# A two-block model kernel: retention's output products moved behind the next head, second weight units by operand tiles, and another order in the mixer

## What is computed

```python
# first block, per layer: h = h + mixer(norm(h)); h = h + cross_attention(norm(h)); h = h + conv_glu_ffn(norm(h))
lru_x, lru_g, m_x, m_o, m_if = split_cols(xn @ cd_w_in, CD_SIZES)      # mixer of layer 1
xc = causal_dwconv(lru_x, ...); gates = sigmoid(xc @ gate_w + gate_b)  # RG-LRU: linear recurrence
u = sqrt(-expm1(2.0 * log_a)) * (i_gate * xc)
h = linear_recurrence(exp(log_a), u) * gelu(lru_g)
xc = silu(causal_dwconv(m_x, ...)); q, k = headwise(xc, ...)           # mLSTM: gated attention, 4 heads
# second block, layer 1: retention
q, k, v = rope(z_q), rope(z_k), z_v                                    # 4 heads, qk 256, v 512 wide
o = rmsnorm(retention(q, k, v), out_norm)
o = o.reshape(B, S, nv) * silu(g)
return o @ w_out
# second block, feed forward
return (silu(h @ w_gate) * (h @ w_up)) @ w_down
```

## Time and profile before

| | |
|---|---|
| median of 3 runs | 3468.95 us (3465.75 to 3472.72) |
| profiled execution, its own time | 3469.26 us |
| its span, first to last instruction | 3467.4 us |
| PE busy | 3201.3 us (92%) |
| DVE busy | 1575.9 us (45%) |
| ACT busy | 1196.1 us (34%) |
| chain that ended last | PE 81%, DVE 12%, ACT 5% |
| mean granted TensorE clock | 0.955 |

### The profile page before, as it was taken

The page is one execution under the profiler, slowest core; times in us unless marked ns, Lnnn a source line. Parts: engine busy times, 40 slices in busy tenths (PEclk is TensorE's granted clock), DMA queues, the critical chain, the costliest instruction groups (busy, mean ns, idle before and its releaser), DMA issues.

```text
span 3467.4 us, 40278 instructions
## 1 busy us (share of the span) xinstructions
PE 3201.3 (92%) x17298; PEld 2530.7 (73%) x17298; DVE 1575.9 (45%) x2043; ACT 1196.1 (34%) x1621; POOL 115.0 (3%) x136
## 2 busy tenths in 40 slices
PE   7889888899999889999998797899999999989999
PEld 6787666678887656778875663678888778768887
DVE  4444456455443476355443426553335423453333
ACT  4343332343322464343223244532224232242221
POOL 1010000000000000000001000000000000000000
PEclk9999999999999999999999897899999999999999
DMA  4343001223332212133322120033323212223331
GB/s 142 112 142 81 20 26 38 73 61 98 99 89 85 77 61 79 43 85 97 97 84 71 55 86 0 22 88 97 97 85 110 73 64 76 85 59 100 98 97 61
DMA packets 344818, 270.34 MB, mean 78 GB/s; under 512 B 17040, under 2 KB 330640, under 8 KB 344384
## 3 DMA queue, kind: packets, MB, share of 16 engines
q1 hardware_dynamic: 340624, 252.30, 24.4%
q0 software_dynamic: 4016, 15.46, 1.3%
HBM read 261.45 MB, written 6.29 MB: 77 GB/s over the span
## 4 chain that ended last, share of the span: by engine, by line
PE 81%; DVE 12%; ACT 5%; issue 1%; POOL 0%; DMA 0%; DVEq 0%; SPq 0%; ACTq 0%; POOLq 0%
PE ps L192 80%; DVE arena L223 3%; DVE arena L215 3%; ACT arena L206 2%; DVE xlo L215 1%; PE ps L195 1%; DVE wlo L215 1%; ACT whi L209 1%; DVE split L215 1%; ACT split L209 1%; DVE sml L232 1%; DVE arena L219 1%; DVE hT L215 1%; ACT L206 0%; ACT arena L209 0%
## 5 line engine op out<-in xcount | busy, mean ns | idle before, releaser
L192 PE MATMUL ps<-xhi,whi 128*128 128x512 f32 (+4 forms) x2192 | 884.8, 404 | 55.5 <-DVE wlo L215 30.5
L192 PE MATMUL ps<-xhi,wlo 128*128 128x512 f32 (+4 forms) x2192 | 862.6, 394 | 0.0
L192 PE MATMUL ps<-xlo,whi 128*128 128x512 f32 (+4 forms) x2192 | 861.3, 393 | 0.0
L192 PE MATMUL ps<-split,whi 128*128 128x512 f32 (+4 forms) x2640 | 832.7, 393 | 26.6 <-DVE split L215 22.2
L215 DVE TENSOR_TENSOR wlo<-wraw,whi 128x2048 fp32r<-128x2048 f32 (+4 forms) x258 | 546.2, 2120 | 499.6 <-ACT whi L209 499.6
L192 PEld LDWEIGHTS ps<-split,whi 128*128 128x128 f32 (+3 forms) x2640 | 492.6, 190 | 157.6 <-issue 31.0
L209 ACT ACTIVATE whi<-wraw 128x2048 fp32r<-128x2048 f32 (+4 forms) x258 | 455.1, 1767 | 403.5 <-PE ps L192 383.5
L192 PEld LDWEIGHTS ps<-xhi,whi 128*128 128x128 f32 (+4 forms) x2192 | 414.1, 189 | 167.6 <-DVE wlo L215 33.9
L192 PE MATMUL ps<-split,wlo 128*128 128x512 f32 (+4 forms) x1320 | 511.4, 387 | 0.0
L192 PEld LDWEIGHTS ps<-xhi,wlo 128*128 128x128 f32 (+4 forms) x2192 | 414.4, 189 | 94.8 <-issue 7.3
L192 PEld LDWEIGHTS ps<-xlo,whi 128*128 128x128 f32 (+4 forms) x2192 | 413.5, 189 | 92.5
(11 more groups left out here) (103 smaller groups left out, 1994.9 us busy)
## 6 DMA issues: line engine op xcount, KB each, us to landing
wraw<-in_ffn_w_up SPq DMA_DIRECT2D x128, 512.0 KB, 5.2
wraw<-in_ffn_w_down SPq DMA_DIRECT2D x32, 1024.0 KB, 5.2
wraw<-in_odd_w_in SPq DMA_DIRECT2D x24, 1024.0 KB, 5.2
wraw<-in_ffn_w_gate SPq DMA_DIRECT2D x44, 512.0 KB, 4.0
wraw<-in_xattn_wkv SPq DMA_DIRECT2D x16, 1024.0 KB, 5.5
wraw<-in_xattn_wq SPq DMA_DIRECT2D x8, 1024.0 KB, 5.3
wraw<-in_xattn_wo SPq DMA_DIRECT2D x8, 1024.0 KB, 5.2
wraw<-in_cd_w_in SPq DMA_DIRECT2D x8, 1024.0 KB, 5.7
```

The lines of the kernel that those rows point to most:

```text
L192: return self.e.matmul(out, lhsT, rhs, start=start, stop=stop, skip_group_check=True)
```

## The change

It makes six edits.

1. In every stage with a `Fresh` norm the second unit too is multiplied by operand tiles: for each k both blocks, instead of all k for one block and then for the other (`fm_tensor`, `i < 2`; `ffn`, `n < 2`). In `mix1` this was so before.
2. All these stages pass `midway`: the unit after the second is split inside the norm's loop, before the fifth high part on ACT and before the sixth product on DVE. In cross attention DVE there also scales the first unit's two blocks (`first_queries`).
3. In GLA the sum of squares stands behind six operand tiles instead of two (`sum_at=6`).
4. In `mix1` the x blocks take any of the eight banks; the gate rows ("if") are projected behind x, ahead of m; the exponentials for lambda stand behind the norm on ACT; exp and tanh change places and buffers in the RG-LRU part.
5. In `mix1` the mLSTM convolutions write `xc_m` (parts of `og`, and `iv`) instead of `hh`, so that they no longer wait for the RG-LRU scans, and the pauses place them and the heads 0 to 2 in earlier rounds.
6. In `odd` the output products of head `hd - 1` stand behind the `o` products of head `hd`, with two sets of `oo` buffers. On DVE their additions to `hT` stand between the steps of the gating chain. ACT splits a further unit ahead of the squares.

```diff
-        def fm_tensor(pe, S, units, src, made, N=T, of=range(8), fresh=None, fine=False, by_tiles=1):
+        def fm_tensor(pe, S, units, src, made, N=T, of=range(8), fresh=None, fine=False, sum_at=2):
...
-                for group in [blocks] if fresh and i < by_tiles else [[b] for b in blocks]:
+                for group in [blocks] if fresh and i < 2 else [[b] for b in blocks]:
...
-                        if early and k == 2:
+                        if early and k == sum_at:
                             early.sum(pe)
...
-                norm.vector(dve)
-                for key, _, _ in units[0][3]:
-                    dve.wait_ge(S.P.of(*key), norm.root())
-                    dve.tt(qq[:, key[1] * T:(key[1] + 1) * T], ps.ap(*key), norm.rs, ALU.mult).then_inc(
-                        *up(S.V, *key, frees=key))
+
+                def first_queries():
+                    W.rest(dve, units[1][0])
+                    for key, _, _ in units[0][3]:
+                        dve.wait_ge(S.P.of(*key), norm.root())
+                        dve.tt(qq[:, key[1] * T:(key[1] + 1) * T], ps.ap(*key), norm.rs, ALU.mult).then_inc(
+                            *up(S.V, *key, frees=key))
+
+                norm.vector(dve, first_queries)
...
-                    for cols in [both] if n == 0 else [both[0:1], both[1:2]]:
+                    for cols in [both] if n < 2 else [both[0:1], both[1:2]]:
...
-                norm.vector(dve)
+                norm.vector(dve, lambda: W.rest(dve, ("up", 1)))
...
-                norm.scalar(act)
+                norm.scalar(act, lambda: W.round(act, ("up", 1)))
...
-                for _ in fm_tensor(pe, S, u_qk, X8, norm.made, fresh=norm):
+                for _ in fm_tensor(pe, S, u_qk, X8, norm.made, fresh=norm, sum_at=6):
...
+            xc_m = [og[:, T:2 * T], og[:, 2 * T:3 * T], og[:, 3 * T:4 * T], iv]
...
-                    yield from fm_tensor(pe, S, u_x, X8, norm.made, of=of_dense, fresh=norm, by_tiles=2)
-                    yield from fm_tensor(pe, S, u_m, X8, norm.made, of=of_dense)
+                    yield from fm_tensor(pe, S, u_x, X8, norm.made, fresh=norm)
...
-                    yield from fm_tensor(pe, S, u_g + u_o, X8, norm.made, of=of_dense)
+                    yield from fm_tensor(pe, S, u_m + u_g + u_o, X8, norm.made, of=of_dense)
...
-                together(project(), lru(), values(), gates(), head(0, 10, 11, 12, 14, 16), head(1, 12, 13, 15, 17, 20),
-                         head(2, 13, 14, 16, 19, 21), head(3, 17, 18, 19, 21, 24))
+                together(project(), lru(), values(), gates(), head(0, 10, 10, 11, 13, 15), head(1, 11, 11, 12, 15, 17),
+                         head(2, 12, 12, 13, 16, 18), head(3, 17, 18, 19, 21, 24))
...
-                    conv4(dve, S, mraws[hd], hh, "mlstm_conv", hd, S.A.of("m", hd), *(
-                        [S.P.of("uT")] if hd == 3 else [S.P.of("i_gate", 3)] if hd == 0 else [S.V.of("lru_scan", 3)]))
+                    conv4(dve, S, mraws[hd], xc_m[hd], "mlstm_conv", hd, S.A.of("m", hd), S.P.of("uT") if hd == 3 else NEVER)
...
-                together(project(), gates(), lru(), head(0, 9, 11, 12, 15, 17), head(1, 11, 13, 15, 18, 21),
-                         head(2, 12, 14, 16, 20, 22), head(3, 13, 18, 19, 22, 25))
+                together(project(), gates(), lru(), head(0, 6, 10, 11, 14, 16), head(1, 7, 11, 12, 16, 18),
+                         head(2, 8, 12, 13, 17, 19), head(3, 9, 18, 19, 22, 25))
...
-                together(project(), values(), lru(), gates(), head(0, 9, 10, 11, 14, 16, 17), head(1, 11, 12, 13, 17, 20, 21),
-                         head(2, 12, 13, 14, 19, 21, 22), head(3, 14, 17, 18, 21, 24, 25))
+                together(project(), values(), lru(), gates(), head(0, 9, 10, 10, 13, 15, 16), head(1, 9, 11, 11, 15, 17, 18),
+                         head(2, 9, 12, 12, 16, 18, 19), head(3, 10, 17, 18, 21, 24, 25))
...
-            oo = [als() for _ in range(4)]
+            oo = [[als() for _ in range(4)] for _ in range(2)]
...
-                    if hd:
-                        for _ in add_tensor(pe, S, outs[hd - 1], oo, [P] * 4, lambda k: S.V.of("o", hd - 1, k)):
-                            pass
                     for _ in tm_tensor(pe, S, u_v[hd], X8, norm.made):
...
                     sum_squares(3)
-                for _ in add_tensor(pe, S, outs[3], oo, [P] * 4, lambda k: S.V.of("o", 3, k)):
+                    if hd:
+                        for _ in add_tensor(pe, S, outs[hd - 1], oo[(hd - 1) % 2], [P] * 4, lambda k: S.V.of("o", hd - 1, k)):
+                            pass
+                for _ in add_tensor(pe, S, outs[3], oo[1], [P] * 4, lambda k: S.V.of("o", 3, k)):
                     pass
...
-                    if hd:
-                        for _ in add_vector(dve, S, outs[hd - 1]):
-                            pass
...
+                    adds = iter(())
+                    if hd:
+                        adds = add_vector(dve, S, outs[hd - 1])
+                    else:
+                        W.rest(dve, u_qk[1][0][0])
                     for d in range(4):
                         o = ot[d % 2]
+                        if d:
+                            next(adds, None)
...
+                    W.round(act, outs[hd - 1][0][0] if hd else u_qk[1][0][0])
...
-                        act.wait_ge(S.V.of("gated", hd, d), S.P.of(f"out{hd - 1}", 7) if hd else NEVER)
-                        act.copy(oo[d].hi, ot[d % 2]).then_inc(*up(S.A, "ohi", hd, d))
+                        act.wait_ge(S.V.of("gated", hd, d), S.P.of(f"out{hd - 2}", 7) if hd > 1 else NEVER)
+                        act.copy(oo[hd % 2][d].hi, ot[d % 2]).then_inc(*up(S.A, "ohi", hd, d))
+                    if hd:
+                        for _ in add_scalar(act, S, outs[hd - 1]):
+                            pass
```

85 lines of the change are left out of this document (42 added, 43 removed).

## The result

| | before | changed |
|---|---|---|
| median | 3469.2 us (4 runs, 3465.75 to 3472.72) | 3387.78 us (4 runs, 3384.33 to 3389.72) |
| ratio | | 0.9764, 95% interval 0.9747 to 0.9781 |
| span of the profiled execution | 3467.4 us | 3386.6 us |
| mean granted TensorE clock | 0.955 | 0.969 |

The account below looks back on a forecast made before the run. TensorE, busy 92% of the span, bounds the kernel, so only its idle time and half clock can be won. 44.1 + 21.5 + 6.6 + 9.6 + 3.4 - 0.8 = 84.4 us off gave 3385 us, 80% between 3371 and 3404.

Parts of the forecast that it names:

- Retention: Retention's second q/k units (28.1 us), last output products (14.5) and stage start (1.5) lose their waits and half clock: 44.1 us gained.
- the cover's slack: Retention: next q/k unit ready some 21 us after the last sum, 1.5 to 2.3 us before 22.50 us of output products end.
- rival (B): Retention's output products do not cover the gating chain and split; 19 us of the gain lost: 3404 us, chance 0.11.
- Mixer: Mixer stage: waits at the second x unit, before q0 and at head 1 shrink or go, less new costs: 21.5 us gained.
- The two terms of -1.5: Mixer: wait at `i_gate` 2 grows from 1.83 to about 3.3 us (-1.5), with half clock behind it (-1.5).
- the later 1.83: Mixer, head 1: TensorE's wait of 1.83 us for ACT goes with 1.7 us of half clock, silu being earlier: +3.5.
- The first estimate of the x unit's cause: Mixer, second x unit: x blocks in all eight banks end the 11.43 us wait for a bank; 15.0 us lost before.
- rival C': Mixer: each table load holds ACT another 1.28 us beyond its record, 7.7 us on six loads: 3393 us, chance 0.03.
- GLA: GLA's start: six tiles ahead of the sum, full clock there, second unit ends at 44 instead of 50.7: 6.6 us gained.
- GLU: Two conv-GLU stages: the 3.36 us wait for `wlo` and half clock go, a 1.7 us wait comes: net 4.8 each.
- SwiGLU: SwiGLU's two stages: a wait of 1.18 us and 0.5 of small waits go, 1.7 each: 3.4 us gained.
- Cross attention: Cross attention's wait before the scores ends 0.1 us later in the first stage, 0.7 in the second: -0.8 us.

## Why the prediction was right

**Retention**, 44.1 forecast, 44.4 measured, and 42.9 with this edit alone: sizes and places are as argued. The term that was off is the cover's slack. I took 21 us for chain and split against 22.5 of output products; the trace has 0.15 us between the low half's end and its use, and the run with doubled subtractions leaves room for 0.6 at most. The unit is ready 22.6 us and not 21 after the products begin. What I left out is seen in the chain: between the first tile and the first addition DVE also makes a `wlo` of 2.29 us, for the second unit of the output products, which my list of the chain did not have. That no wait came is luck as much as working: rival (B) was much nearer than its 0.11 said, and 1 us more in the chain would have brought its waits. (B) was also sized wrongly. It counts four places, but only three have the cover: the q/k units of heads 2 and 3 and the last output products. Head 1's unit was split earlier, by the prediction's own account. At those three the run with doubled subtractions lost 3.6 us each for 2.2 of wait.

**Mixer**, 21.5 forecast, 16.2 measured. Between the same matmuls in both traces it falls into three parts:

| part of the stage | forecast | measured |
|---|---|---|
| start to `i_gate` 2 | 15.0 - 1.5 - 1.5 = 12.0 | 14.4 |
| `i_gate` 2 to q0 | 6.0 | 5.5 |
| q0 to the end | 3.5 | -3.7 |

The second x unit took 10.90 us at clock 1.00, as forecast, and the wait at the gate rows was 0.78 (1.3 forecast). The two terms of -1.5 did not come: the wait at `i_gate` 2 stayed at 1.83 and did not grow to 3.3, since behind its two loads ACT still stood 0.79 us for m0's block. The wait before q0 was 3.93 (3.9 forecast), but the closeness is luck: the prediction's own numbers, 18.5 less 14.9, give 3.6. The trace has 18.4 us from m3's copy to q0, of which TensorE is busy for 14.5.

The step that failed is "the later 1.83 goes with its 1.7 us of half clock: +3.5, since heads 1 and 2 have their silu a round or more earlier". It is off by 7.2 us, of which the -1.5 terms hid a part. The silus did come earlier and that wait did go, but I followed only ACT into these rounds. The PSUM bank of `M` of head 1 is freed by DVE, and TensorE now has 24 dense matmuls between the `M` of head 0 and that of head 1, where it had 48: 5.85 us of wait, and a stretch of 10.2 us at half clock that begins in it. The runs show that DVE's order is the cause. Moving TensorE's matmul gains 0.9 us in the stage. Moving DVE's product for head 0 takes the wait away and brings one of 2.60 at the next head (0.4 us gained), and moving it for heads 0 to 2 leaves none: 9.0, 6.1 and 8.6 us gained in the three runs that have it. These three also have cross attention 0 changed ahead of the mixer, so how much of the figure is clock was not separated.

**The first estimate of the x unit's cause** was half right. The 15.0 us came, but the banks alone give 8.4.

**Table loads** (rival C'). ACT on the way to q0 in the changed kernel (timeline): the load for the exponentials behind m3's copy, the one for the tanhs, then a load and the square roots, a load and the silus.

```profile
1179.27 1.28 ACT L200 ACT_TABLE_LOAD   x1
...
1184.86 1.28 ACT L206 ACT_TABLE_LOAD   x1
...
1191.58 1.28 ACT L206 ACT_TABLE_LOAD   x1
1192.87 2.19 ACT L206 ACTIVATE arena<-arena 128x512 f32<-128x512 f32 x4
1195.08 1.28 ACT L206 ACT_TABLE_LOAD   x1
1196.37 1.67 ACT L206 ACTIVATE arena<-arena 128x512 f32<-128x512 f32 x3
```

On this chain the next activation starts at most 0.02 us behind each load, the load at most 0.02 us behind what precedes it, and 1.28 us a load is all that they cost. The prediction speaks of six loads on the chain, but its own list has four, and so has the trace: ahead of m3's copy ACT stands still for 3.68 us, so that the earlier loads delay nothing. With four, the rival's price is 5.1 us and not 7.7. The drain of about 1.38 us that the Trainium skill names (ScalarE: Activation LUTs, "What ACT_TABLE_LOAD costs") doesn't show on this chain; for four loads it would be an estimated 5.5 us more.

**GLA**, 6.6 forecast, 5.5 measured: full clock at the sum (1.98 us against 3.78 before), and the wait of 2.36 (2.3 forecast). The sum began at 26.84 and not at 26.3 or earlier: TensorE's first matmul came 0.2 us later in this execution, which is outside the stage's length, and the transposes behind it took 5.79 us and not 5.49, which is inside it. **GLU**, 4.8 each forecast, 4.2 and 4.3 measured, with the wait moved by one unit and 1.66 us long (1.7 forecast). **SwiGLU**, 3.4 forecast, 3.1 measured. **Cross attention**, -0.8 forecast, -0.2 measured. Its wait at the scores stayed, as forecast, and for the reason given: the split ahead of the products ate what their place gained. The experiments put numbers on it: without the move 10.42 us, with it behind the split 5.58, ahead of the split 0.96. What I treated as a loss to accept was some 10 to 13 us to be had in the two stages.

**The sum** was 84.4 us and 81.4 was measured (80.8 in the spans). The mixer's missing 5.3 and 1.6 net in the other terms are partly filled by 3.4 us in stages whose code did not change, which no step had foreseen. That the sum came within 3 us is luck in this part; without those 3.4 us the time would have been some 3391, still in the range.

## What to carry to other kernels

Where a move brings one engine's work forward, look up who frees the PSUM bank it will take next, and follow that engine's queue too: the wait moves to the last engine that was not followed. If moving the waiting instruction only moves the wait, change the order on the engine that it waits for; the products of three heads placed in that engine's idle time ahead of late splits were worth 6 to 9 us, where the first head's alone gave 0.4, and two lines exchanged in the norm's pause some 5 us in each of two stages. Edits that move a split into a loop and edits that change the order in which its tiles are used should be judged as one: alone, each made SwiGLU 0 slower than before.
